# Expert weights w3 on ScalarE's DMA queue, w1 and w2 on SyncE's

## The reference

```python
group_logits = (u @ w_group + b_group);  g_idx = argmax(group_logits)     # 4 groups
top_v, top_i = top_k(expert logits within the group, 2)                    # 8 experts in a group
combine = sum(one_hot(g_idx * 8 + top_i, 32) * softmax(top_v) * p_sel)
y = zeros_like(u)
for e in range(32):
    hid = silu(u @ w1[e]) * (u @ w3[e])        # w1[e], w3[e]: 1024 x 256
    y = y + combine[:, e:e + 1] * (hid @ w2[e])  # w2[e]: 256 x 1024
return h + y
```

## Time and profile before

| what | value |
|---|---|
| median of three executions | 648.66 us |
| profiled execution: its own time | 650.51 us |
| profiled execution: span | 648.9 us |
| PE busy | 583.6 us (90%) |
| ACT busy | 226.8 us (35%) |
| DVE, POOL busy | 238.5 us, 137.7 us |
| DMA traffic | 136.16 MB, of which q1 carries 124.92 MB |

### The profile page before, as it was taken

How to read it: one execution, slowest core, us unless ns; L and a number is a source line. 1 busy time by engine, 2 the same in 40 slices (tenths; PEclk the granted TensorE clock), 3 DMA queues, 4 the chain that set the end, 5 groups by cost and what they waited for, 6 DMA issues and landing times.

```text
span 648.9 us, 9042 instructions
## 1 busy us (share of the span) xinstructions
PE 583.6 (90%) x3499; PEld 399.1 (62%) x3499; DVE 238.5 (37%) x552; ACT 226.8 (35%) x431; POOL 137.7 (21%) x224
## 2 busy tenths in 40 slices
PE   8799999998999997999999959999999997768840
PEld 7688778895666563666888626555565555445520
DVE  3644335234554864385736711111111110011106
ACT  6725415252645443774515602112212121111110
POOL 8100001110232211234300011332223331222110
PEclk9799799998999997999999989999999999999995
DMA  8910000007000004000878597999999999999939
GB/s 254 388 63 1 0 2 0 1 2 277 1 1 1 0 5 135 1 2 0 321 286 365 205 349 272 367 392 384 394 377 385 382 388 391 389 389 398 371 108 348
DMA packets 35820, 136.16 MB, mean 210 GB/s; under 512 B 8808, under 2 KB 10904, under 8 KB 26816
## 3 DMA queue, kind: packets, MB, share of 16 engines
q1 hardware_dynamic: 29536, 124.92, 50.7%
q0 software_dynamic: 5664, 8.55, 4.3%
q10 hardware_dynamic: 576, 2.10, 0.8%
HBM read 131.28 MB, written 12.65 MB: 222 GB/s over the span
## 4 chain that ended last, share of the span: by engine, by line
PE 80%; DMA 7%; DVE 6%; issue 4%; ACT 2%; SPq 1%; POOL 0%; ACTq 0%; POOLq 0%; DVEq 0%
PE ps L2104 18%; PE ps L1775 16%; PE ps L2129 9%; PE ps L1961 5%; PE ps L1851 5%; PE ps L2066 5%; PE ps L1906 5%; PE ps L1950 5%; DMA w_in_ffcq<-in_w_in 2%; DMA yg<-y_rows 2%; PE ps L2116 2%; DMA h_rows<-x 2%; PE ps L1926 1%; DMA xg<-h_rows,idx 1%; PE ps L1711 1%
## 5 line engine op out<-in xcount | busy, mean ns | idle before, releaser
L2104 PE MATMUL ps<-w,xt 128*64 128x256 f32 x1024 | 120.0, 388 | 18.3 <-issue 17.1
L2104 PEld LDWEIGHTS ps<-w,xt 128*64 128x64 f32 x1024 | 78.0, 140 | 69.3 <-issue 39.8
L1649 DVE TENSOR_TENSOR xt<-ps,g_ffn_c 128x512 f32<-128x512 f32 x32 | 22.1, 692 | 206.8 <-PE ps L2066 206.8
L2129 PE MATMUL ps<-w,hT 128*64 128x512 f32 x256 | 61.8, 604 | 0.0
L1195 ACT ACTIVATE hsb<-ps,row_scale 128x256 f32<-128x256 f32 x32 | 15.2, 474 | 130.8 <-PE ps L2104 130.8
L840 POOL DMA_INDIRECT xg<-h_rows,idx x32 | 30.4, 949 | 116.5 <-PE ps L2066 109.5
L830 POOL DMA_INDIRECT y_rows<-yh,idy x32 | 32.7, 1022 | 77.7 <-ACT yh L1212 77.7
L770 POOL TENSOR_SCALAR_AFFINE_SELECT probT<-probT 128x128 f32<-128x128 f32 (+2 forms) x80 | 23.5, 312 | 92.2 <-ACT probT L1115 91.5
L1961 PE MATMUL ps<-probT,vals 128*128 128x512 f32 (+4 forms) x160 | 42.6, 410 | 0.0
L1950 PE MATMUL ps<-qT,kT 68*128 68x400 f32 (+9 forms) x160 | 42.1, 407 | 0.0
L2066 PEld LDWEIGHTS ps<-ident,xg 64*128 64x128 f32 x256 | 30.6, 199 | 17.5 <-issue 17.5
(11 more groups left out here) (309 smaller groups left out, 940.7 us busy)
## 6 DMA issues: line engine op xcount, KB each, us to landing
w<-in_w SPq DMA_DIRECT2D x96, 1024.0 KB, 26.1
yg<-y_rows SPq DMA_DIRECT2D x4, 1024.0 KB, 7.8
x<-in_x SPq DMA_DIRECT2D x4, 512.0 KB, 5.5
w_in_v<-in_w_in SPq DMA_DIRECT2D x1, 2048.0 KB, 12.3
w_in_k<-in_w_in SPq DMA_DIRECT2D x1, 2048.0 KB, 17.3
w_in_q<-in_w_in SPq DMA_DIRECT2D x1, 2048.0 KB, 22.0
w_oa<-in_w_o SPq DMA_DIRECT2D x1, 2048.0 KB, 8.8
w_ob<-in_w_o SPq DMA_DIRECT2D x1, 2048.0 KB, 8.3
```

Source lines behind the costliest of these rows:

```text
L2104: ins = pe.matmul(ps[j * slots:(j + 1) * slots, 2 + b, 0:F], xt[b][:, k, :], w13[s][:, j, k, :], start=(k == 0), stop=(k == DK - 1))
L2129: ins = pe.matmul(ps[q * slots:(q + 1) * slots, 6 + b, :], hT[b][:, m, :], w2s[s][:, m, q * 512:(q + 1) * 512], start=(m == 0), stop=(m == ...
```

## The change

For the reloaded experts 7 to 31, w3 is no longer issued by SP. ACT issues it, right after the copy of the hidden rows of the expert whose slot it fills, at which point expand of that expert is done. SP still issues w1 and w2 with the same waits. Tiles, semaphores and their counts, sizes and everything that PE, DVE and POOL do stay as they are.

```diff
@@ load_w13(e), SyncE
                 s = e % RING
                 sp.wait_ge(h13_done, e - RING + 1)
                 sp.dma_start(w13[s][:, 0, :, :], w1_v[e]).then_inc(w13_in[s], 16)
-                sp.dma_start(w13[s][:, 1, :, :], w3_v[e]).then_inc(w13_in[s], 16)
@@ copy_hidden(e), ScalarE
                 act.activation(hsb[b][:, :], ps[:, 2 + b, 0:F], ACT.Copy, scale=row_scale[:, e:e + 1]
                                ).then_inc(hs_out, 1)
+                if e + RING < NE:
+                    s = e % RING
+                    act.dma_start(w13[s][:, 1, :, :], w3_v[e + RING]).then_inc(w13_in[s], 16)
```

## The result

The changed kernel is slower: 655.18 us in the median (654.71 to 655.28, four executions), against 648.57 us, a ratio of 1.0088 (95% interval 1.0065 to 1.0111). A second timing gave 1.0068 (1.0046 to 1.0090). The profiled execution took 655.28 us with a span of 653.7 us, against 650.51 and 648.9 us: 4.8 us more in both. The forecast was 651.8 us, 3.2 us more. The medians differ by 6.6 us, twice the forecast. 1.8 us of that come from which execution was profiled: before, it took 1.94 us more than the median, after the change 0.10 us more. In the second timing the medians are 655.15 and 650.04 us, 5.1 us apart.

The account below looks back on a forecast made before the run. Saturated weight transfers were taken to bound the kernel. Loss at the end 3.1 us, plus 0.3 for clock, minus 0.2 gained, made 3.2 us: 648.66 to 651.8 us; own range 650.2 to 653.6, whole range 646.5 to 655.5 us.

Parts of the forecast that it names:

- Bound: Experts: transfers saturated all along at 386 to 387 GB/s; PE uses up its lead, then waits 17.1 us in total.
- ACT's issue: Between `hsb` and silu: 0.35 us per w3 load, falling in 0.91 us of ACT idling, so nothing on the path.
- The rival in which ACT is held by SP's full queue: Reloads: ACT's issues take up to 8.00 us, the end moves by up to 27 us, 660 us or more; chance 0.08.
- What the prediction said of SP: SP's queue: 25 loads fewer to issue, worth nothing in time; its issues were to get shorter.
- Turns of the two queues and the lead of w3: Experts: queues alternate by packet, w3 runs six experts ahead (16.1 us), first wait at expand(14), last w3 in by about 586 us.
- The loss at the end: Experts 26 to 31: w1 and w2 alone take 6.11 us, PE needs 6.71; start 31 is 3.1 us late, bounds 1.8 and 4.2.
- Clock: Behind expert 26: an expand slowed by the 1.2 GHz clock after a long wait would count; 0.3 us put on it.
- The 0.2 us gained by an expand(31) without a wait: Last expert: expand(31) takes 3.45 us for 3.69 us when no wait precedes it, 0.2 us gained.
- Tail: After start 31: PE's chain, scatter, `yg` loads and stores stay as long as before; nothing waits for w2(31).
- No change: Whole kernel: saturated engines carry the same bytes, so the time stays 648.7 us; chance 0.27.
- Faster by a higher rate: Expert transfers: two rings keep each engine fuller; 3% more rate gives about 645 us; chance 0.12.

Follow-up runs that it names:

- g1: Kernel before, with SP holding back w2(5), w3(6) and w2(6) until the gather of expert 0 has landed; ratio 0.9950 against the kernel before.
- e4: Kernel before, but ACT issues w2 of reloaded experts 7 to 31 and SP only w1 and w3; ratio 1.0101 against the kernel before.
- e1: Changed kernel, but w3 of experts 25 to 31 stays on SP, so ACT issues w3 of 7 to 24; ratio 1.0024 against the kernel before.
- e2: Changed kernel, but ACT issues w3 of experts 25 to 31 only and SP all other loads; ratio 1.0045 against the kernel before.
- e3: Changed kernel, but w3 of experts 30 and 31 stays on SP, so ACT issues w3 of 7 to 29; ratio 1.0023 against the kernel before.
- e6: Changed kernel, but ACT issues w3 of experts 29, 30 and 31 only; ratio 1.0027 against the kernel before.
- a1: The changed kernel unchanged, timed and profiled again; ratio 1.0068 against the kernel before.
- e5: Kernel before, but ACT issues w2 of experts 7 to 29, while SP issues w2 of 30 and 31 after the loop; ratio 1.0067.
- g2: Kernel before, with SP holding back only w3(6) and w2(6) until the gather of expert 0 has landed; ratio 0.9954 against the kernel before.

## Why the prediction was right, and where it was off

The direction and the mechanism came as forecast. The size did not: 655.18 us lies outside the forecast's own range of 650.2 to 653.6 us and just inside the whole range. The upper end of that, 655.5 us, had been drawn for a dropped clock and some holding of ACT, and neither of them set the end. So it is in part luck that the whole range holds the result. The second timing is nearer: +0.68%, with the forecast's 0.5% inside its interval.

*Bound.* Right. The rate stayed at 389 GB/s with PE waiting in the middle, and g1 shows that transfer time saved ahead of the experts comes out at the end.

*ACT's issue.* Right: 0.335 us in the median, 0.386 us at most, at the same time as `hsb`, and never held back while SP was. The rival in which ACT is held by SP's full queue is out. What the prediction said of SP is wrong: its issues did not get shorter but longer (4.4 against 2.9 us in the mean, at most 12.17 against 8.00 us), since its loads get only a part of the turns now. SP was not on the path, so nothing hung on it.

*Turns of the two queues and the lead of w3.* Right. The first wait came at expert 15, forecast 14, and the last w3 was in by 586 us as forecast. e4 adds a condition the prediction lacked, the size of the packets: w3, with 7.2 KB a packet in the mean against 5.0 KB on q1, got its lead, and w2, with 3.8 against 7.3 KB, got none.

*The loss at the end.* Right in its mechanism, shown by e1, e2 and e3 in trace and time, and by e6 in the trace, each against a loss in proportion to the loads moved. The term was too small: 3.1 us forecast with an upper bound of 4.2, 4.42 us measured from expand(13) on (3.95 in a1). Of the 1.3 us, 0.5 us are in PE's pace, 34.05 us from start 26 to 31 and not 33.6, since in the chain an expand behind even a short wait takes 3.67 and not 3.45 us. 0.17 us of it is only how the chain counts a start. The other 0.8 us are in the arrival for expert 26, at 587.1 us (with the 0.43 us taken off by which expand(13) starts later) and not 586.3. From 394 to 440 us the rate was 367 GB/s, against 374; 46 us of that are 0.32 MB, about 0.8 us. But part of this is the later start already taken off: with the window moved by the same 0.43 us the rate is 369 GB/s, and about 0.6 us are left. Why is not settled, and the second queue need not be the cause: e3, with two queues, had 373 GB/s there, and e2, with one at that time, 371.

*What was not foreseen.* PE's 5.9 us of waits before `contract`. w2(e-1) stands behind w1(e) in a queue that then gets only a part of the turns. They fall where PE has to wait anyway: after 588 us there is no such wait.

*Clock.* One expand at 562.51 us took 5.22 us, at expert 23, hidden by the waits behind it. So the 0.3 us for it were not spent. The 0.2 us gained by an expand(31) without a wait are there in the chain (3.48 for 3.69 us) but too fine to be seen in the time.

*Tail.* Right, 32.1 us in both.

*No change* was the likelier rival. It falls with the two timings of the change, and with e2 and e6: the order of arrival is worth something although the bytes and their rate are the same. The rule of the Trainium skill ("DMA: Bandwidth & Descriptors", section "Issuing engines are not separate DMA queues") that issuing from several engines only saves the time of issuing holds here for the rate, 389 against 386 GB/s, but not for the order of arrival, and so not for the time. *Faster by a higher rate* falls with 389 against 386 GB/s.

## What to carry to other kernels

Where the transfers are the bound, ask not only how many bytes there are, but how many are still behind the load that the compute engine waits for. The end is the latest, over the last steps, of a step's arrival plus the compute that must follow it. A second queue can change that order: here its loads ran ahead, and the steps at the end were left with transfers (6.1 us) shorter than their compute (6.7 us), so the compute ended late. No order with two queues was faster here than all loads in one queue in the order of use. And before a gather on which a whole stage hangs, try holding back loads that have time: here that gave 0.5%.

## What the runs showed of the hardware

- Two full queues shared the DMA engines by packets and not by bytes: 2806 against 2800 packets but 20.42 against 10.77 MB in 90 us (e4).
- SP was held in an issue for up to 12.17 us while ACT's issues of the same size took 0.39 us at most, so a full queue of SP did not hold ACT. ACT can be held too: in e4 and e5, where the loads in its own queue waited longer (14.2 to 50.7 us from issue to landing in e5), its issue took 0.37 us at first and from 517 us on up to 2.98 and 4.23 us.
- The first gather of an expert's rows took 8.3 us from issue to use behind a full queue, 6.9 us to landing with two loads held back (g2) and at most 3.9 us with three (g1).
- The kernel's time varies by up to 5 us between executions on one chip (647.4 to 652.4 us in 29 executions of the kernel before beside e1 to e4). In the profiles a part of that lies ahead of the experts (expand(13) at 473.8 to 478.3 us). A single profile resolves a change of this size only when it is counted from a point behind that start.
